# Gate and up superblocks 1 to 8 with seven Strassen products for eight on two pairs of K tiles, in a one-layer decoder trunk

## What is computed

```python
x = x + 0.5 * swiglu(rmsnorm(x, norm_ffn1), w1_gate, w1_up, w1_down)
h = rmsnorm(x, norm_mix);  q, k, v, u = split(h @ w_in)
x = x + concat(attention(rope(q), rope(k), v), pool_mixer(u)) @ w_out
x = x + 0.5 * swiglu(rmsnorm(x, norm_ffn2), w2_gate, w2_up, w2_down)
out = rmsnorm(x, norm_final)

def swiglu(h, w_gate, w_up, w_down):          # w_gate, w_up: 2048 x 5632
    return (silu(h @ w_gate) * (h @ w_up)) @ w_down
```

## Time and profile before

| | |
|---|---|
| median of 3 runs | 1738.09 us (1737.96 to 1738.16) |
| span of the profiled execution | 1736.5 us |
| TensorE matmuls | 1727.4 us busy, 99%, 7734 matmuls |
| VectorE | 1149.5 us busy, 66% |
| ScalarE | 788.1 us busy, 45% |
| GpSimd | 19.6 us busy, 1% |
| DMA | 334.51 MB moved, 193 GB/s on average |

### The profile page before, as it was taken

How to read it: one execution, slowest core, us unless ns; L and a number is a source line. 1 busy time by engine, 2 the same in 40 slices (tenths; PEclk the granted TensorE clock), 3 DMA queues, 4 the chain that set the end, 5 groups by cost and what they waited for, 6 DMA issues and landing times.

```text
span 1736.5 us, 20290 instructions
## 1 busy us (share of the span) xinstructions
PE 1727.4 (99%) x7734; PEld 1433.8 (83%) x7734; DVE 1149.5 (66%) x1491; ACT 788.1 (45%) x907; POOL 19.6 (1%) x24
## 2 busy tenths in 40 slices
PE   9999999999999999999999999999999999999998
PEld 7888888888888888888888888888888888888886
DVE  7766666666665566587877886666666666654554
ACT  6544444444444444454554554444444444443443
POOL 0000000000000000000040000000000000000000
PEclk9999999999999999999999999999999999999999
DMA  8656555565555555666544566656566565655552
GB/s 292 205 193 192 193 192 193 191 193 193 193 197 193 193 193 193 216 203 193 169 156 159 194 194 194 194 193 193 193 193 193 193 193 193 209 203 194 194 194 97
DMA packets 174945, 334.51 MB, mean 193 GB/s; under 512 B 6136, under 2 KB 18352, under 8 KB 174768
## 3 DMA queue, kind: packets, MB, share of 16 engines
q1 hardware_dynamic: 172960, 332.51, 58.5%
q10 hardware_dynamic: 1936, 1.32, 0.2%
HBM read 331.71 MB, written 2.10 MB: 192 GB/s over the span
## 4 chain that ended last, share of the span: by engine, by line
PE 99%; DMA 0%; ACT 0%; SPq 0%; DVE 0%; issue 0%; ACTq 0%; DVEq 0%
PE banks L437 31%; PE banks L439 31%; PE banks L438 31%; PE banks L456 2%; PE banks L423 2%; PE banks L426 1%; DMA raw<-in_w_gate 0%; PE banks L577 0%; PE banks L601 0%; PE banks L589 0%; PE banks L623 0%; PE banks L621 0%; PE banks L619 0%; PE banks L603 0%; PE banks L517 0%; ACT w_hi L722 0%
## 5 line engine op out<-in xcount | busy, mean ns | idle before, releaser
L996 DVE TENSOR_TENSOR w_lo<-raw,w_hi 128x1024 fp32r<-128x1024 f32 x622 | 763.4, 1229 | 551.5 <-ACT w_hi L722 549.4
L722 ACT ACTIVATE w_hi<-raw 128x1024 fp32r<-128x1024 f32 x622 | 658.1, 1060 | 905.1 <-PE banks L439 875.9
L437 PE MATMUL banks<-w_hi,act 128*128 128x512 f32 x1536 | 598.3, 390 | 0.0
L439 PE MATMUL banks<-w_lo,act 128*128 128x512 f32 x1536 | 597.6, 389 | 0.0
L438 PE MATMUL banks<-w_hi,act 128*128 128x512 f32 x1536 | 597.5, 389 | 0.0
L438 PEld LDWEIGHTS banks<-w_hi,act 128*128 128x128 f32 x1536 | 288.3, 188 | 60.1
L439 PEld LDWEIGHTS banks<-w_lo,act 128*128 128x128 f32 x1536 | 288.3, 188 | 59.7
L437 PEld LDWEIGHTS banks<-w_hi,act 128*128 128x128 f32 x1536 | 288.3, 188 | 59.6
L437 PE MATMUL banks<-w_hi,h 128*128 128x512 f32 x832 | 323.8, 389 | 0.0
L439 PE MATMUL banks<-w_lo,h 128*128 128x512 f32 x832 | 323.7, 389 | 0.0
L438 PE MATMUL banks<-w_hi,h 128*128 128x512 f32 x832 | 323.7, 389 | 0.0
(11 more groups left out here) (135 smaller groups left out, 466.2 us busy)
## 6 DMA issues: line engine op xcount, KB each, us to landing
raw<-in_w_down SPq DMA_DIRECT2D x88, 1024.0 KB, 5.0
raw<-in_w_gate SPq DMA_DIRECT2D x84, 1024.0 KB, 5.1
raw<-in_w_up SPq DMA_DIRECT2D x84, 1024.0 KB, 5.2
raw<-in_w_in SPq DMA_DIRECT2D x32, 1024.0 KB, 5.5
raw<-in_w_out SPq DMA_DIRECT2D x16, 1024.0 KB, 5.0
raw<-in_w_up SPq DMA_DIRECT2D x8, 512.0 KB, 9.9
raw<-in_w_gate SPq DMA_DIRECT2D x7, 512.0 KB, 9.9
xr<-in_x SPq DMA_DIRECT2D x8, 256.0 KB, 9.0
```

The lines of the kernel that those rows point to most:

```text
L437: pe.matmul(dst, operand[:, k, hi], w_hi[:, s, w], start=k == first, stop=False)
L439: mm = pe.matmul(dst, operand[:, k, hi], w_lo[:, s, w], start=False, stop=k == last)
L722: act_e.activation(w_hi[:, s, :], raw[:, (p // 2) % RAW_SLOTS, off:off + PIECE], ACT.Copy).then_inc(hi_ready, 1)
L996: dve.tensor_tensor(w_lo[:, s, :], raw[:, (p // 2) % RAW_SLOTS, off:off + PIECE], w_hi[:, s, :].bitcast(F32), ALU.subtract).then_inc(lo_re ...
```

## The change

Of superblocks 1 to 8 of each FFN, K tiles 0 to 3 are computed in another way, as a 2x2 block product. The left matrix has the activations' blocks A11, A12 (tokens 0 to 127, K tiles 0 and 1, K tiles 2 and 3) and A21, A22 (tokens 128 to 255). The right matrix has the weights' blocks: B11 and B21 are the gate's columns, B12 and B22 the up's. Eight block products become seven, by Strassen's method in Winograd's form:

- The sums of activations (S5 = A21 - A22, S2 = A11 - S5, S7 = A21 - A11, S12 = A12 - S2) are made once per FFN on VectorE (`make_forms`, behind piece 13 of superblock 0), rounded on ScalarE (`round_forms`, ahead of the first silu) and split on VectorE (`split_forms`).
- The four sums of weights are made per superblock: `first_sums` on GpSimd makes two, 128x1024 each (gate + up into `sums`, and up's halves in place), `add_sum` on VectorE the other two, behind pieces 9 and 10.
- A superblock has 20 pieces. Pieces 0 and 1 are B11's two K tiles (512 columns, 3 matmuls each). Pieces 3, 5, 7, 9, 11, 13 are products of two K tiles against one set of activations (6 matmuls each). Six pieces of K tiles 4 to 15 of the gate stand between them (2, 4, ... 12) and six of the up behind them (14 to 19), 12 matmuls each, with `rows_of` as before.
- The products use PSUM banks 4 to 7 as well. ScalarE copies bank 4 out (`copy_p1`), VectorE combines the products in six passes of 128x512 behind pieces 15, 16 and 17 (`fold_v`, `fold_v_n`, `fold_gate`). Silu now stands behind all 20 pieces and reads `gu` (`silu_fast`). In the next superblock VectorE adds the up banks to `folds` behind piece 2 (`merge`) and multiplies behind piece 4 (`merged_product`).
- In all superblocks and both FFNs the 16 transposes become one of 128x1024 (`square_h`), which stays within each 32 partitions, behind piece 13 (piece 4 in the superblocks of the old kind and in `down`). The squares are then moved to their partitions by 16 DMAs of 32 KB from SBUF to SBUF on SyncE's queue (`exchange`), behind the superblock's eighth load, or the seventh in the old kind and in `down`. `turned` has another order inside, and `round_h` and `split_h` read it with other strides; in fast superblocks they stand behind pieces 17 and 18.
- The hardware loop has four turns of two fast superblocks each, because chunks sit two slots further on in every second one (`shift`); superblocks 9 and 10 are written out behind it.

```diff
+FAST_SBS = 8
+FAST_PIECES = 20
...
+B11_0, B11_1, B21, T1, T3, B22, T2, T4 = 0, 1, 3, 5, 7, 9, 11, 13
+GATE_AT = {2: 4, 4: 6, 6: 8, 8: 10, 10: 12, 12: 14}
+UP_AT = {14 + n: 4 + 2 * n for n in range(6)}
+SUMS = (T1, T3, T2, T4)
+S5, S7, S2, S12 = range(4)
+P1_BANK, N5_BANK, N7_BANK, R6_BANK = 4, 5, 6, 7
+FAST_SLOTS = (0, 1, 2, 3, 2, 3, 0, 1)
...
+FAST_FREE = (-6, -4, -2, 0, 5, 9, 12, 12)
+COPY_P1_AT, ROUND_FAST_AT = 8, 17
+FOLD_AT = (15, 16, 17)
+MERGE_AT, PRODUCT_AT, SQUARE_H_AT, SPLIT_FAST_AT = 2, 4, 13, 18
...
+            def exchange(n, dst):
+                sp.wait_ge(h_squared, n + 1)
+                for q in range(SB):
+                    for c in range(SB):
+                        for_half = dst[c * SQ:(c + 1) * SQ, :, :, :].rearrange(
+                            "p (t q) k j -> p t q (k j)", q=SB)[:, :, q, :]
+                        sp.dma_start(for_half, squared[q * SQ:(q + 1) * SQ, c, :, :]
+                                     .rearrange("p (t k) j -> p t (k j)", k=SB)).then_inc(h_turned, 16)
 
...
+                for c, (part, kc) in enumerate((("gate", 0), ("up", 0), ("gate", 1), ("gate", 2),
+                                                ("gate", 3), ("up", 1), ("up", 2), ("up", 3))):
+                    slot = (FAST_SLOTS[c] + shift) % RAW_SLOTS
+                    sp.wait_ge(lo_ready, first + FAST_FREE[c])
+                    sp.dma_start(raw[:, slot, :].rearrange("p (t n) -> p t n", n=QCOLS),
+                                 f[part][kc * 4 * P:(kc + 1) * 4 * P, bass.ds(i * QCOLS, QCOLS)]
+                                 .rearrange("(t p) n -> p t n", p=P)).then_inc(raw_landed[slot], 16)
+                exchange(fi - 1, turned)
...
+            def add_product(bank, hi, lo, s, j, first, last):
+                dst, w = banks[:, bank, :], slice(j * QCOLS, (j + 1) * QCOLS)
+                pe.matmul(dst, hi, w_hi[:, s, w], start=first, stop=False)
+                pe.matmul(dst, lo, w_hi[:, s, w], start=False, stop=False)
+                return pe.matmul(dst, hi, w_lo[:, s, w], start=False, stop=last)
...
+            def fast_gate_up(f, i, shift):
+                first, fi = fast_first(f, i), f["sb"] + i
+                pe.wait_ge(silu_ready, fi)
+                for p in range(FAST_PIECES):
+                    pe.wait_ge(lo_ready, first + p + 1)
+                    if p in (B11_0, B11_1):
+                        mm = tile_product(p, 0, p, 0, P1_BANK, p == B11_0, p == B11_1)
+                    elif p in GATE_AT:
+                        k = GATE_AT[p]
+                        for t in range(2):
+                            mm = rows_of(t, p % SPLIT_SLOTS, GATE_BANK, act, (k, k + 1), 4,
+                                         (KT - 1, KT)[t])
+                    elif p in UP_AT:
+                        k = UP_AT[p]
+                        for t in range(2):
+                            mm = rows_of(t, p % SPLIT_SLOTS, UP_BANK, act, (k, k + 1),
+                                         (KT, 4)[t], KT - 1)
+                    elif p == B21:
+                        for j in range(2):
+                            mm = tile_product(p, j, 2 + j, 0, GATE_BANK, False, False)
+                    elif p == T1:
+                        pe.wait_ge(forms_ready, f["fast"] // FAST_SBS + 1)
+                        mm = form_product(p, S5, N5_BANK, True, True)
+                    elif p == T3:
+                        mm = form_product(p, S7, N7_BANK, True, True)
+                    elif p == B22:
+                        pe.wait_ge(product_ready, fi)
+                        mm = form_product(p, S12, UP_BANK, True, False)
+                    elif p == T2:
+                        mm = form_product(p, S2, R6_BANK, True, True)
+                    else:
+                        for j in range(2):
+                            mm = tile_product(p, j, 2 + j, 1, GATE_BANK + 1, False, j == 1)
+                    mm.then_inc(piece_used, 1)
 
...
+            def round_fast(turn, first, nth, p, shift):
+                act_e.wait_ge(piece_used, first + p - SPLIT_SLOTS + 1)
+                if p in SUMS:
+                    act_e.wait_ge(summed, 4 * nth + SUMS.index(p) + 1)
+                if p in (T1, T4):
+                    dst, src = w_hi[:, p % SPLIT_SLOTS, :], sums[:, :]
+                else:
+                    c = FAST_CHUNK[p][0]
+                    slot = (FAST_SLOTS[c] + shift) % RAW_SLOTS
+                    act_e.wait_ge(raw_landed[slot], (turn + (1 if c < 4 else 2)) * 16)
+                    off, size = fast_part(p)
+                    dst, src = w_hi[:, p % SPLIT_SLOTS, 0:size], raw[:, slot, off:off + size]
+                act_e.activation(dst, src, ACT.Copy).then_inc(hi_ready, 1)
+            def copy_p1(first, fi):
+                act_e.wait_ge(piece_used, first + B11_1 + 1)
+                act_e.wait_ge(product_ready, fi)
+                act_e.activation(folds[:, 1, :], banks[:, P1_BANK, :],
+                                 ACT.Copy).then_inc(p1_copied, 1)
+            def silu_fast(merges):
+                act_e.wait_ge(folded, merges + 1)
+                for t in range(2):
+                    ins = act_e.activation(gu[:, t, :], gu[:, t, :], ACT.Silu,
+                                           scale=r_col[:, t:t + 1])
+                ins.then_inc(silu_ready, 1)
+            def fast_gate_up(f, i, shift):
+                turn, first, fi = f["turn"] + 2 * i, fast_first(f, i), f["sb"] + i
+                nth = f["fast"] + i - 1
+                for p in range(FAST_PIECES):
+                    round_fast(turn, first, nth, p, shift)
+                    if p == COPY_P1_AT:
+                        copy_p1(first, fi)
+                    if p == ROUND_FAST_AT:
+                        round_h(fi - 1, SB * i - SB, turned)
+                silu_fast(merges_of(f, i))
 
...
-            def turn_h(n, dst, step):
+            def square_h(n):
 
                 dve.wait_ge(product_ready, n + 1)
-                ins = turn_squares(dst, gu, 2 * step, 2)
-                if step == TURN_STEPS - 1:
-                    ins.then_inc(h_turned, 1)
+                dve.transpose(squared[:, :, :, :].rearrange("p c m j -> p m c j"),
+                              gu[:, :, :].rearrange("p t (k c i) -> p (t k) c i", c=SB, i=SQ))\
+                   .then_inc(h_squared, 1)
 
...
+                dve.wait_ge(whole_act_ready, f["fast"] // FAST_SBS + 1)
+                a11, a21 = (whole[:, 0:2, t, :] for t in range(2))
+                a12, a22 = (whole[:, 2:4, t, :] for t in range(2))
+                s5, s7, s2, s12 = (raw_forms[:, n, :, :] for n in range(4))
+                form_stepped(dve.tensor_tensor(s5, a21, a22, ALU.subtract))
+                form_stepped(dve.tensor_tensor(s2, a11, s5, ALU.subtract))
+                dve.tensor_tensor(s7, a21, a11, ALU.subtract)
+                dve.tensor_tensor(s12, a12, s2, ALU.subtract).then_inc(raw_forms_ready, 1)
...
+            def add_sum(nth, p, shift):
+                high = slice(PIECE, 2 * PIECE)
+                gate, up = raw[:, FAST_SLOTS[0] + shift, :], raw[:, FAST_SLOTS[1] + shift, :]
+                if p == T2:
+                    dve.wait_ge(summed, 4 * nth + 2)
+                    dst, a, b = up[:, high], sums[:, :], up[:, high]
+                else:
+                    dve.wait_ge(summed, 4 * nth + 3)
+                    dst, a, b = sums[:, :], up[:, high], gate[:, high]
+                dve.tensor_tensor(dst, a, b, ALU.add).then_inc(summed, 1)
...
+            def merge(first, merges):
+                dve.wait_ge(piece_used, first)
+                dve.wait_ge(folded, merges)
+                dve.tensor_tensor(folds[:, :, :], banks[:, UP_BANK:UP_BANK + 2, :], folds[:, :, :],
+                                  ALU.add).then_inc(merged, 1)
...
+            def fold_v(first, nth):
+                dve.wait_ge(piece_used, first + T2 + 1)
+                dve.wait_ge(p1_copied, nth + 1)
+                dve.tensor_tensor(folds[:, 0, :], banks[:, R6_BANK, :], folds[:, 1, :],
+                                  ALU.subtract).then_inc(fold_step, 1)
+            def fold_v_n(nth):
+                dve.wait_ge(fold_step, 3 * nth + 1)
+                dve.tensor_tensor(gu[:, 1, :], banks[:, N7_BANK, :], folds[:, 0, :], ALU.add)
+                dve.tensor_tensor(folds[:, 0, :], banks[:, N5_BANK, :], folds[:, 0, :],
+                                  ALU.add).then_inc(fold_step, 1)
+            def fold_gate(first, nth):
+                dve.wait_ge(piece_used, first + T4 + 1)
+                dve.wait_ge(fold_step, 3 * nth + 2)
+                dve.tensor_tensor(gu[:, 0, :], banks[:, GATE_BANK, :], folds[:, 1, :],
+                                  ALU.add).then_inc(fold_step, 1)
+                dve.tensor_tensor(gu[:, 1, :], banks[:, GATE_BANK + 1, :], gu[:, 1, :],
+                                  ALU.subtract)
+                dve.wait_ge(fold_step, 3 * nth + 3)
```

(95 more changed lines are left out.)

236 lines of the change are left out of this document (163 added, 73 removed).

## The result

The changed kernel takes **1776.88 us** (median of 4 runs, 1776.08 to 1778.17) against 1738.10 before: 1.0224 times as long, 95% interval 1.0211 to 1.0236. I had forecast 1716.7 and a range up to 1729. The profiled execution spans 1775.8 us, where my sum was 1715.1.

What follows compares the result with a forecast made beforehand. PE was taken as the bound, busy 1727.4 of 1736.5 us. Profiled execution 1736.5 - 21.8 (fewer matmuls) + 0.4 (forms) = 1715.1 us; keeping the median run's 1.6 above that span gave 1716.7, range 1715 to 1729.

Steps and rivals of the forecast that it cites:

- The saving: On PE in 16 fast superblocks: 96 matmuls fewer at 0.2266 us each, 21.8 us, if PE stays fed.
- the price of an exchange issue: On SyncE's queue: each of 16 SBUF transfers holds it 0.37 us, 5.9 us per exchange, at no cost.
- my own formula, 32.4 + 16 i: Landing time in us of the next superblock's third load at issue price i; wanted by 41.2.
- Rival 2: SyncE's queue becomes the bound: at 0.7 us per issue the third load is late by 2.4 us, 1755 us; 11%.
- the threshold of 0.55: On SyncE's queue: issue price in us from which the next superblock's third load is late.
- GpSimd beside VectorE: Splits beside GpSimd's adds in fast superblocks take up to 0.6 us more, covered by time to spare: no cost.
- rival 1: GpSimd and VectorE exclude each other: late adds lose 0.6 to 1.1 us per superblock, 1727 to 1734 us; 8%.
- The start of FFN 1: Making the forms delays VectorE's splits and silu around superblock 0's end: 0.4 us taken, bounds 0 to 1.5.
- the transpose of 128x1024: On VectorE, one in place of sixteen of 436 ns: 1.3 us taken, between 1.2 and 1.74.
- ScalarE's waits at round_h: ScalarE waits 2.4 us per fast superblock for the exchange to land; split 18 still in time, no cost.
- rival 4: PE's short pieces stall about as much as is saved, 1.4 us per superblock: 1738 us; 6%.
- rival 3: Longer loop bodies are fetched again at backward branches, 2.6 us each, 16 us: 1732 us, or 1742; 7%.

Runs made afterwards that it cites:

- e4: Changed kernel, complete, with the transpose behind piece 8 instead of 13 and the 16 transfers issued earlier, eight after the sixth load, eight after the eighth: 1722.30 us.
- e3: Kernel before with one transpose and 16 transfers per superblock in place of 16 transposes, no Strassen products: 1738.25 us, 1.0001 of before.
- e9: e4 with GpSimd's adds held until VectorE has split the third piece: 1741.57 us, 1.0019 of before.
- e2: Changed kernel with GpSimd's two sums per superblock covering 32 columns instead of 1024 (result not right): 1751.83 us, 1.0089 of before.
- e7: Changed kernel with each transfer one 1 KB run per partition instead of two of 512 bytes (h in another order): 1771.85 us, 1.0197 of before.
- e6: Changed kernel with the alterations of e1 and e2 together (result not right): 1717.94 us, 0.9884 of before.
- e1: Changed kernel with 4 transfers of 128 KB per transpose instead of 16 of 32 KB, squares not changing partitions (h not right): 1722.54 us, 0.9913 of before.
- e5: e4 with GpSimd's first adds of each FFN waiting for VectorE's third split of superblock 1: 1721.92 us.
- e8: Changed kernel with sixteen 436 ns transposes on VectorE again and no transfers: 1738.99 us, 1.0005 of before.

## Why the prediction was wrong, point by point

**The saving** was right: 96 matmuls, 0.2267 us each, a steady fast superblock of 42.16 us in e4 where I had 42.2.

**The step that failed is the price of an exchange issue.** I took 0.37 us, the price of a load from HBM and of the 64 KB ident load; it was 0.60 at the median, 0.64 from start to start, in the changed kernel as in e3 and e4 (6 of the changed kernel's 352 took 0.76 to 1.77). With i = 0.64 my own formula, 32.4 + 16 i, gives 42.6 against a latest landing of 41.2: 1.4 us late, where 1.8 was measured. Rival 2 was the right mechanism, at the right place, and I gave it 11%, for a wrong reason: I tied a high price to a crowded queue and judged the queue not to be crowded. Its size was short, though: 16 x 1.4 = 22 us on my forecast make 1739, and the kernel took 1776.9, because the next two terms came on top. No row of before had a transfer with both ends in SBUF, so 0.37 to 1.24 were bounds, and the threshold of 0.55 lay inside them. That should have weighed more, and the range should have reached 1755.

**GpSimd beside VectorE** was the second mis-sized term. The earlier trace rows show a split stretched by 0.6 us, and I took that as the price. It was the rest of a short operation, not a small share of it. GpSimd's timeline in the kernel before, beside the split of 1.79 us that starts at 882.88:

```profile
882.55 1.04 POOL L1457 TENSOR_TENSOR window<-window 128x508 f32<-128x508 f32 x1
883.65 1.07 POOL L1456 COPY window<-window 128x8 f32<-128x8 f32 x1
```

The split ends at 884.67, 1.08 us after GpSimd's add has ended (883.59), and the copy of 8 columns, which waits in its turn, takes 1.07 us where those of 2 and 4 columns before it took 0.19. In the changed kernel p2's split ends 1.09 us after the add. So the trace of before already agreed with waiting for a whole instruction. Beside 128x1024 adds of 2.4 us three splits take 6.83 or 6.3 us for 2.4, and two at the merge 5.38 for 2.4. My rival 1 had this right, and the Trainium skill ("SBUF — State Buffer", section "SBUF: two separate sides") states it: a VectorE operation with two SBUF inputs and a GpSimd operation that reads SBUF exclude each other for the whole instruction. The runs agree, down to the merge that is not held up (1.22 us in e9), and where I wrote that the trace shows less than a whole wait I had misread it. The rival's condition, that the adds come late, was then made true by the queue. I had counted the two rivals as separate cases; they were one chain.

**The clock.** I had no term for it, and gave no reason. The steady superblocks of the changed kernel have 14 waits of 2.4 to 3.4 us in front of p2. Behind seven of them matmuls ran at the lower level for a while and lost 1.7 us or more; behind the other seven, of the same lengths (2.8 us at 247 us, 3.4 at 1173), they did not. Of 14 such waits in e2, 13 of them at most 2.2 us, only the one of 3.4 lost more than the 0.1 us of a restart. In e7 five of 14 were followed by such a stretch, one of 2.2 us among them (at 151.94), and one of 3.35 us (at 1120.27) was not. With the restarts that makes 17.7 us in the changed kernel and 5 in e2. What decides between equal waits stays open.

**The start of FFN 1**: I took 0.4 us and gave 1.5 as a bound. Counted as under e6, it cost 4.9 us in e1 and 3.7 in e4: the first three splits of superblock 1 met GpSimd's first adds. e6 against e1 shows that 4.0 us of it are the adds, e5 that moving them inside the start only moves the wait. The 0.9 us that e6 leaves bound the forms' own part (e6 also zeroes `sums` there); my walk had left out two passes of VectorE in front of the split of p0, `split_forms` (1.22 us) and the zeroing of `folds` (0.91 us). FFN 2 had no such wait, as forecast.

**What held**: the transpose of 128x1024 took 1.24 us (1.3); GpSimd's adds 2.4 (2.1 to 2.6); ScalarE's waits at round_h were 98.1 us in 16 (I had 2.4 each), and covered but for 0.5 us of TensorE's in each of the first two superblocks (at 95.92 and 143.50); the short products (rival 4) starve nobody, e4; the loops' longer bodies (rival 3) are not fetched again: the instruction queue moved 0.70 MB, which is what 7638 - 6 x 372 = 5406 matmuls at 131 bytes make.

## What to carry to other kernels

A DMA that is moved onto a queue costs its issue time (here 0.6 us) in front of all that is queued behind it; count the loads behind it back from when they are wanted, and put transfers that nobody is in a hurry for where the next load still has to wait anyway. A price with no row of its own gets its range, and if the verdict turns inside that range, the forecast has to say so with its chances. Work for GpSimd on SBUF operands, as the adds here, is time taken from VectorE's operations with two SBUF inputs, so it belongs beside pieces that have that much to spare. And where a row shows an operation stretched by a neighbour, look at when the neighbour ended: the stretch can be the rest of a short one, and grows with its length.

## What the runs showed that I had not expected

- An issue of an SBUF to SBUF transfer on SyncE's queue costs 0.60 us at 32 KB and 0.62 at 128 KB, against 0.37 for a 1 MB load from HBM, in two shapes of access, also where hardly anything but the exchange itself moves (51 to 56 GB/s from 180 to 186 us in the changed kernel).
- GpSimd and VectorE alternate by whole operations: beside 2.4 us adds the split of h, 1.22 us alone, took 3.41 (e8), and an add waited as well (3.39 us).
- Of 14 equal-looking waits of 2.4 to 3.4 us on TensorE, half were followed by a stretch at the lower clock (granted 0.50) that cost 1.7 us or more, and half by none.
